# State-space stretch: angles summed ahead of the low halves on GpSimd, sines on ScalarE, paired input products, modulation sums gathered in PSUM

## What is computed

```python
lam_bar = jnp.exp(lam * step)
b_bar = ((lam_bar - 1.0) / lam)[:, :, None] * b_mat
bu = jnp.einsum('bsgc,gnc->bsgn', u.astype(jnp.complex64), b_bar)
a = jnp.broadcast_to(lam_bar[None, None], (1, s_, SSM_GROUPS, SSM_STATE))
_, states = lax.associative_scan(_ssm_combine, (a, bu), reverse=reverse, axis=1)
c_mat = lax.complex(c_re.astype(jnp.float32), c_im.astype(jnp.float32))
return jnp.real(jnp.einsum('bsgn,gcn->bsgc', states, c_mat))
...
y_ssm = (y_fwd + y_bwd).reshape(b_, s_, SSM_WIDTH) + ssm_d[l] * ug.reshape(b_, s_, SSM_WIDTH)
y_act = jax.nn.gelu(y_ssm, approximate=False)
```

```python
shift, scale, gate = jnp.split(s_lat @ w_mod[layer] + b_mod[layer], 3, axis=-1)
shift_c, scale_c, gate_c = jnp.split(s_ctx @ w_mod[layer] + b_mod[layer], 3, axis=-1)
```

## Time and profile before

| what | value |
|---|---|
| runs | 4009.96 us median of 3 (4005.93 to 4010.44) |
| the profiled execution | 4007.19 us, of which its span is 4005.4 us |
| TensorE busy | 3835.0 us, 96% of the span |
| VectorE busy | 2413.7 us, 60% |
| ScalarE busy | 1674.4 us, 42% |
| GpSimd busy | 804.3 us, 20% |
| mean DMA rate over the span | 174 GB/s |
| TensorE in slices 2 to 6 of 40 (100 to 600 us) | 90% or more in each |
| VectorE in the same slices | 90% or more in four, in the fifth 70 to 80% |

### The profile page before, as it was taken

The page is one execution under the profiler, slowest core; times in us unless marked ns, Lnnn a source line. Parts: engine busy times, 40 slices in busy tenths (PEclk is TensorE's granted clock), DMA queues, the critical chain, the costliest instruction groups (busy, mean ns, idle before and its releaser), DMA issues.

```text
span 4005.4 us, 75139 instructions
## 1 busy us (share of the span) xinstructions
PE 3835.0 (96%) x31164; PEld 3601.1 (90%) x31164; DVE 2413.7 (60%) x3405; ACT 1674.4 (42%) x2349; POOL 804.3 (20%) x595
## 2 busy tenths in 40 slices
PE   7999999999999988999999999999999999999997
PEld 6777778899999988999999999999799999989887
DVE  5999977643777767555555555543333333657556
ACT  4223236644455576333444334432222223243674
POOL 4878774034400000000000000000000002113223
PEclk9999999999999999999999999999999999999999
DMA  5887774355455544555665555522522223223333
GB/s 210 305 304 279 298 294 147 127 191 189 160 192 195 189 138 144 194 193 191 223 226 210 197 201 191 197 106 95 179 95 102 95 97 127 95 74 138 117 106 136
DMA packets 142750, 695.21 MB, mean 174 GB/s; under 512 B 44384, under 2 KB 54752, under 8 KB 62816
## 3 DMA queue, kind: packets, MB, share of 16 engines
q1 hardware_dynamic: 89952, 641.77, 44.6%
q10 hardware_dynamic: 52608, 50.74, 3.8%
HBM read 672.54 MB, written 19.92 MB: 173 GB/s over the span
## 4 chain that ended last, share of the span: by engine, by line
PE 79%; DVE 13%; ACT 3%; issue 3%; DMA 1%; POOL 1%; ACTq 0%; DVEq 0%; SPq 0%; POOLq 0%
PE banks L430 50%; PE banks L2264 17%; DVE w_lo L402 2%; PE banks L2334 1%; DVE pq L1365 1%; PE banks L2170 1%; DVE banks L1355 1%; PE banks L2437 1%; DVE banks L1342 1%; PE banks L2503 1%; PE banks L2478 1%; DVE oh L1605 1%; DVE rq L1401 1%; ACT gw L747 1%; ACT w_hi L394 1%
## 5 line engine op out<-in xcount | busy, mean ns | idle before, releaser
L430 PE MATMUL banks<-h_hi,w_hi 128*128 128x256 f32 x6432 | 1640.8, 282 | 54.1 <-DVE w_lo L402 16.2
L430 PE MATMUL banks<-h_hi,w_lo 128*128 128x256 f32 x6432 | 1615.9, 278 | 0.0
L430 PE MATMUL banks<-h_lo,w_hi 128*128 128x256 f32 x6432 | 1615.5, 278 | 0.0
L394 ACT CAST w_hi<-ring 128x1024 fp32r<-128x1024 f32 x986 | 984.8, 1048 | 1033.4 <-PE banks L430 445.4
L402 DVE TENSOR_TENSOR w_lo<-ring,w_hi 128x1024 fp32r<-128x1024 f32 x810 | 1003.4, 1271 | 518.7 <-ACT w_hi L394 514.5
L430 PEld LDWEIGHTS banks<-h_hi,w_hi 128*128 128x128 f32 x6432 | 1141.9, 190 | 103.3 <-issue 86.0
L430 PEld LDWEIGHTS banks<-h_hi,w_lo 128*128 128x128 f32 x6432 | 1139.7, 189 | 1.2 <-issue 0.2
L430 PEld LDWEIGHTS banks<-h_lo,w_hi 128*128 128x128 f32 x6432 | 1139.8, 189 | 0.0
L402 POOL TENSOR_TENSOR w_lo<-ring,w_hi 128x1024 fp32r<-128x1024 f32 x176 | 446.9, 2544 | 1602.6 <-ACT w_hi L394 1601.2
L2264 PE MATMUL banks<-wp_hi,w_hi 128*128 128x256 f32 x2048 | 566.8, 277 | 5.2 <-DVE wp_lo L1638 5.1
L2264 PE MATMUL banks<-wp_hi,w_lo 128*128 128x256 f32 x2048 | 566.1, 276 | 0.0
(11 more groups left out here) (391 smaller groups left out, 4318.8 us busy)
## 6 DMA issues: line engine op xcount, KB each, us to landing
ring<-in_stream_dram SPq DMA_DIRECT2D x555, 1024.0 KB, 4.8
spare<-in_stream_dram SPq DMA_DIRECT2D x30, 1024.0 KB, 5.7
cst<-in_stream_dram SPq DMA_DIRECT2D x23, 1024.0 KB, 6.3
g_in<-g_out ACTq DMA_DIRECT2D x8, 1024.0 KB, 6.4
g_out<-stage ACTq DMA_DIRECT2D x31, 256.0 KB, 2.6
heads_d<-stg ACTq DMA_DIRECT2D x4, 1024.0 KB, 8.3
hb<-heads_d ACTq DMA_DIRECT2D x8, 512.0 KB, 4.0
X<-in_x_in_dram SPq DMA_DIRECT2D x2, 1024.0 KB, 7.2
```

The lines of the kernel that those rows point to most:

```text
L394: act.copy(w_hi[:, t.par, s], weights(t.slot)[:, s]).then_inc(hi_done, 1)
L430: m = pe.matmul(bank(b, e - a, a), w[:, t.par, k], x(k)[:, a:e], start=first and a == 0, stop=last and e == n, skip_group_check=e - a < n)
```

## The change

- The table now holds angles in turns, not sines: `phases_dve` has four instructions (one over both parts of the frequency at once) and `tables` is gone. GpSimd's `rotation` becomes `phase`: add coarse and fine angle, round, subtract, three instructions. ScalarE's new `rotate` makes of them absolute value, sine, and cosine as the sine of a quarter turn minus the absolute value. `rot` has four buffers; `xph` and `aph` have two.
- GpSimd makes both low halves in the stretch, and `phase(u + 4)` stands ahead of them; VectorE makes none.
- `coeffs_dve` has five instructions in place of eight.
- `bu` becomes `bu_pair(u)`, every second unit: the two units' products stand in different row groups of 32, in turn, into banks 4 and 5. It stands behind `ssm_out`, and waits until VectorE has read both banks.
- The 24 copies and turns of the modulation sums become two and one: `csp` is widened with zeros, and the slice that a tile uses is shifted by two rows for every four tiles, so that 16 groups gather in the 32 rows of bank 7. `mods_turn` transposes with eight small products behind the first gate tile, and `mods_read` copies once.

```diff
-            def bu(u):
+            def bu_pair(u):
...
                 if u >= 2:
-                    pe.wait_ge(S("bu_free"), u - 1)
+                    pe.wait_ge(S("bu_free"), u)
...
                 for f in range(2):
-                    m = pe.matmul(bank(4 + u % 2, T, f * T), b_st[s_, c0 % 2, d, f], qku[s_, 20 + c0],
-                                  start=True, stop=True)
-                m.then_inc(S("bu_done"), 1)
+                    for w in range(2):
+                        s_ = slice(32 * (j + w), 32 * (j + w) + 32)
+                        m = pe.matmul(bank(4 + (u + w) % 2, T, f * T), b_st[s_, c0 % 2, d, f], qku[s_, 20 + c0],
+                                      start=True, stop=True)
+                        if f:
+                            m.then_inc(S("bu_done"), 1)
...
-                if q % 4 == 0 and q:
-                    pe.wait_ge(S("mod_out"), q // 4)
+                if q == 64:
+                    pe.wait_ge(S("mod_out"), 1)
                 pe.wait_ge(tile_loaded[t.slot], t.loaded())
+                a = 30 - 2 * (q // 4 % 16)
...
-                if v in (0, 2, 5) and q:
-                    pe.wait_ge(S("mix_read"), d)
-                    mod_turn(q // 4 - 1)
-                if u + 2 < UNITS:
-                    bu(u + 2)
                 if u and u % 2 == 0:
                     ssm_out(u - 2)
+                if u % 2 == 0 and u + 2 < UNITS:
+                    bu_pair(u + 2)
...
+            def rotate(u):
+
+                act.wait_ge(S("xph_ready"), u + 1)
+                if u >= 4:
+                    act.wait_ge(S("pq_ready"), u - 3)
+                x = xph[:, u % 2]
+                act.activation(aph[:, u % 2], x, ACT.Abs).then_inc(S("abs_ready"), 1)
+                act.activation(rot[:, u % 4, 1], x, ACT.Sin, scale=TURN)
+                act.wait_ge(S("abs_ready"), u + 1)
+                act.activation(rot[:, u % 4, 0], aph[:, u % 2], ACT.Sin, bias=V("halfpi"), scale=-TURN)\
+                    .then_inc(S("rot_ready"), 1)
...
+                for v in range(8):
+                    if v in (0, 1, 3, 4, 6):
+                        hi_split(act, mix_low(c0, v))
+                    if 8 * c0 + v + 3 < UNITS:
+                        rotate(8 * c0 + v + 3)
+                    if c0 == 5 and v == 1:
+                        mod_out(0)
+                    if v == 3 and c0:
+                        gelu(c0 - 1)
+                    if v in (0, 2, 3, 5, 6):
+                        mix_out(c0, v)
...
+                if u >= 2:
+                    pool.wait_ge(S("rot_ready"), u - 1)
+                ta, tb = tab[c0 % 2][:, v, 0:16], tab[c0 % 2][:, v, 16:32]
+                pool.tensor_tensor(rt[:, 0], ta.unsqueeze(2).to_broadcast([P, 16, 16]),
+                                   tb.unsqueeze(1).to_broadcast([P, 16, 16]), ALU.add).then_inc(S("rt_ready"), 1)
+                pool.wait_ge(S("rt_ready"), 2 * u + 1)
+                pool.tensor_scalar(rt[:, 1], rt[:, 0], MAGIC, MAGIC, ALU.add, ALU.subtract).then_inc(S("rt_ready"), 1)
+                pool.wait_ge(S("rt_ready"), 2 * u + 2)
+                pool.tensor_tensor(xph[:, u % 2], rt[:, 0], rt[:, 1], ALU.subtract).then_inc(S("xph_ready"), 1)
...
+                if u + 4 < UNITS:
+                    phase(u + 4)
                 if v in (0, 1, 3, 4, 6):
-                    lo_split(pool, mix_low(c0, v), 0)
-                if u + 3 < UNITS:
-                    rotation(u + 3)
+                    for h_ in (1, 0):
+                        lo_split(pool, mix_low(c0, v), h_)
...
-                if v in (0, 1, 3, 4, 6):
-                    lo_split(dve, mix_low(c0, v), 1)
```

More of the change, by code:

```diff
@@ L249, in build @@
         td = place("td", [P, 2, T], F32, TA + 8 * K)
-        tab1 = place("tab1", [P, 2, 8, 32], F32, TA + 14 * K)
+        tab1 = place("tab1", [P, 8, 32], F32, TA + 14 * K)
         tab = [tab0, tab1]
@@ L560, in _, with mod_out @@
                     act.activation(s5w[:, 6:8], s5w[:, 4:6], ACT.Sin, scale=TURN).then_inc(S("s5_act"), 1)
-                if j == 6:
-                    tables(0)
             for j in range(4):
                 hi_split(act, Tile("v", j).next())
-            def mod_out(b):
-                act.wait_ge(mm_done, Tile("mix", MIX * (b // 3) + mix_at((1, 4, 7)[b % 3], 1)).done())
-                if b:
-                    act.wait_ge(S("mod_turned"), b)
-                act.copy(mtmp[:], bank(7)).then_inc(S("mod_out"), 1)
+                if j < 3:
+                    rotate(j)
+            def mod_out(r):
+                act.wait_ge(mm_done, (Tile("mix", MIX * 5 + mix_at(1, 1)), Tile("mix", MIX * 7 + mix_at(7, 1)))[r].done())
+                act.copy(modrows[:, r], bank(7)).then_inc(S("mod_out"), 1)
             def mix_out(c0, v):
@@ L1106, in _, with phase @@
             pool.wait_ge(S("h_pool"), 2)
-            def rotation(u):
+            def phase(u):
                 c0, v = u // 8, u % 8
@@ L1126, in _ @@
+                pool.wait_ge(S("rt_ready"), 2 * u + 2)
+                pool.tensor_tensor(xph[:, u % 2], rt[:, 0], rt[:, 1], ALU.subtract).then_inc(S("xph_ready"), 1)
             for j in range(4):
                 lo_split(pool, Tile("v", j).next(), 0)
-                if j < 3:
-                    rotation(j)
+                phase(j)
+            pool.wait_ge(lo_done[1], N0["mix"] + 1)
             for u in range(UNITS):
                 c0, v = u // 8, u % 8
+                if u + 4 < UNITS:
+                    phase(u + 4)
@@ L1306, in _ @@
                     dve.wait_ge(S("s5_act"), 1)
-                    dve.tensor_copy(csp[:, :, 0:2], cs[:]).then_inc(S("mix_in"), 1)
+                    dve.tensor_copy(csp[:, :, 30:32], cs[:]).then_inc(S("mix_in"), 1)
+                    L(dve.tensor_tensor(pick[:], C("ident", 0, 32), C("ident", 32, 64), ALU.add))
+                    for n in (64, 96):
+                        L(dve.tensor_tensor(pick[:], pick[:], C("ident", n, n + 32), ALU.add))
                 if j == 3:
```

128 lines of the change are left out of this document (43 added, 85 removed).

## The result

| | before | changed |
|---|---|---|
| median | 4010.2 us (4 runs, 4005.93 to 4011.64) | 3952.63 us (4 runs, 3950.52 to 3958.06) |
| profiled execution | 4007.19 | 3950.52 (span 3948.7) |
| first dense tile of `mix` to first gate tile | 108.03 to 585.75: 477.7 | 106.72 to 523.67: 416.95 |

The ratio is 0.986, 95% interval 0.9843 to 0.9877: faster by 57.6 us, where 53 were forecast.

What follows compares the result with a forecast made beforehand. TensorE's own work was taken as the floor, VectorE just above it. 408.2 + 11 + 3.4 + 2 = 424.6 us against 477.7, with -1.1 and +1.8 a saving of 52.4: 3957 us predicted, range 3938 to 3988.

Steps and rivals of the forecast that it cites:

- The floor: From first dense tile of `mix` to first gate tile, TensorE's own work falls from 457.8 to 408.2 us.
- Pairs: 31 input-product pairs on TensorE: 1.2 us each, 37.2 in all, saving 28.5; bounds 1.06 and 2.12 each.
- VectorE's relief: In the stretch, taking work from VectorE alone could win at most 19.9 us of waiting and slow clock.
- The meeting in unit 4: Before the v = 6 and 7 pair, TensorE waits 2.2 us for VectorE, five cycles: 11; bounds 0, 26.
- The sign that went with it: TensorE's idle time stands before the pair of v = 6 and 7, naming VectorE's multiply, not the low half.
- Five buffers: In the last two cycles, D2's late load makes TensorE wait 1.7 us twice: 3.4, bounds 0 and 6.
- The slow clock: Slow clock behind TensorE's waits in the stretch: 2 us.
- The engines: In the stretch, GpSimd busy about 325 us, VectorE about 335, DMA share near 0.88; GpSimd's `tensor_scalar` taken as 0.7.
- Rival A: No waits remain: VectorE's table meets no half, five buffers suffice; 14 us more gained, 3942 us; chance 0.15.
- Rival C: Loads and the two engines' meeting eat the shorter cycle; at 330 GB/s 19 us more, 3976; chance 0.18.
- Rival B: TensorE's input pairs don't overlap: 28 us more, 3985 us; chance 0.10.
- Rival D: GpSimd becomes the bound by its unseen `tensor_scalar`: passes today's cycle at 3.1 us, at 4 gives 4069; chance 0.03.

Runs made afterwards that it cites:

- b_vector: Changed kernel's work for VectorE, GpSimd and ScalarE's sines, but TensorE's single input products and 24 turns kept as in the kernel before: 4008.0 us, ratio 0.9993.
- a_in_turn: Changed kernel with a pair's products issued unit by unit, both of the first unit and then both of the second: 3960.0 us.
- a_spaced: Changed kernel with the five dense tiles of a cycle spread more evenly among the modulation tiles: 3953.2 us.
- a_table3: Changed kernel with three of the four table instructions executed three times, in seven cycles: 4012.3 us.
- b_tensor: Kernel before with only the two TensorE parts, input products in pairs and modulation sums gathered and turned once: 4052.8 us, ratio 1.0106.

## Why the prediction was right, point by point

- **The floor.** TensorE's own work was priced at 408.2 us. The cycles without a wait bear it out to 0.3 us, in the changed kernel (51.1 against 50.9) and in b_vector (57.5 against 57.2).
- **Pairs.** Taken at 1.2 us, measured 1.06 to 1.07: 4.0 us mis-sized. I stayed with the column groups' row. The Trainium skill ("TensorEngine Tiling (Array Packing)", Key Properties) states that different tiles can load weights and multiply in parallel, and that was the better price. The trace now agrees for row groups, 1.07 against 1.92 us.
- **Why it needed VectorE's relief.** This was understated. The prediction said that taking work from VectorE alone could win at most 19.9; it won 3.3, too little to measure. It did not ask what taking work from TensorE alone would do, and the answer is a loss of 42 us. The parts give -3 and +42, together -58.
- **The meeting in unit 4.** Taken at 11 us (six for the table, in five cycles), 0 in the profiled execution, 4.2 in that of a_in_turn and 1.7 in that of a_spaced. The mechanism is real, but it needs a collision, and I took it for certain in five cycles; in the changed kernel all seven tables of the stretch took 1.9 to 2.4 us. The rule for the wait held: 5.5 + table - 9.3 gives 2.6 us for a table of 6.4 (measured 2.69) and 5.8 for one of 9.6 (measured 5.88). Its bound of 26 was too low all the same: a_table3 shows 54 us in seven cycles, since slow clock follows each wait, which the term left out. The sign that went with it failed too: the idle time of the changed kernel names the low half, and none of it stands before the pair of v = 6 and 7.
- **Five buffers.** Taken at 3.4 us for two waits, bounds 0 and 6; measured 8.6 in five, the longest 4.0. This is the term that was too small: three of the waits stand at D2 as forecast, but one of them comes in a cycle with six buffers, and two more stand elsewhere. The slow clock, taken at 2, is what remains: 416.95 - 404.2 of work (408.2 with pairs of 1.07) - 8.6 = 4.2, which also holds the errors of the prices.
- **The engines.** GpSimd was busy 341 us against 325 forecast, mainly because its `tensor_scalar` took 1.07 and not 0.7. That is within the bounds, but the argument that a one-input operation should not cost more than a two-input one fails: the addition took 0.61. VectorE 322 against 335, the table without collisions; DMA share 0.88 as forecast.
- **Around it.** The stretch begins 1.3 us earlier (1.1 forecast), `mods_turn` takes 1.8 as forecast.

So -4.0 (pairs), -11 (meeting), +5.2 (buffers) and +2.2 (clock) make -7.6, and the stretch was 7.6 below the 424.6. Of that, some 3.6 were lost again in the spread behind it. That the time came within 5 us is partly luck: errors of 15 us one way met 7.4 the other way and 3.6 behind the stretch, and whether a table meets a half was left to when the loads come. Rival A was half right: no table met a half, but six and five buffers did cost waits. Rival C came true only with five buffers: over a whole cycle with seven the loads brought 361 GB/s, not the 330 that it supposed. Rival B falls with the pair. Rival D was close: its threshold was 3.1 us for the unseen operation, and at 3.2 the run was slower than before.

## What to carry to other kernels

When one engine's program is the floor and another lies just above it, price each half of a change alone: less work for the first can be a loss until the second has room at the place where they meet. A batched issue that waits for two buffers at once saves time on the issuing engine but makes such a place; put the consumer's long side jobs into the longest interval between two batches, which here was worth 35 us for one moved call and 52 for two. And count a wait of TensorE by what follows too: in a_table3 each wait of some 5 us cost about 2.5 more in slow clock.

## What was not expected of the hardware

- TensorE ran products of different row groups side by side even where the four instructions of one group stood before those of the other: 1.07 us for eight instructions in either order, and 1.92 in one row group.
- A VectorE instruction that reads two operands from SBUF, or a short `tensor_scalar`, grew to about the length of the GpSimd subtraction under way: 2.51 us in a_in_turn (L1263) instead of 0.42 to 0.58 in the changed kernel, and 2.35 instead of 0.29 in a_table3, while L1331, which reads one operand from PSUM, took 0.68 to 0.69 all 64 times. The Trainium skill ("SBUF — State Buffer", Who interferes with whom) states that a VectorE instruction with two SBUF inputs contends with a GpSimd instruction that reads SBUF, and that the shared port pair is an exclusive lock. The rows agree.
- GpSimd's `tensor_scalar` of 256 elements with two operations (add, subtract) took 1.07 us, against 0.61 for its two-input addition of the same size.
- A wait of 5.88 us was followed by twelve us at a granted clock of 0.72; in b_tensor, with waits of up to 12.1 us, the mean of the stretch was 0.91.
